# Trainium2, one core: a fused two-block transformer kernel, its opening re-queued and re-ordered, and the forget gates of the second block computed first

## The reference

```
mod = silu(c) @ w_mod + b_mod              # 9 shifts, scales and gates per layer, for x and for ctx
x += 0.5 * gate * swiglu(rms_norm(x) * (1 + scale) + shift)        # and the same for ctx
x += gate * mixing(rms_norm(x) * (1 + scale) + shift)   # Fourier, neighbourhood, gated linear, grouped-query
x += 0.5 * gate * swiglu(...)
```

```
h += out(mixing(rmsnorm(h)))     # 4 softmax pairs with forget gates, 4 retention heads
h += swiglu(rmsnorm(h))
```

## Time and profile before

| | us |
|---|---|
| median of 3 runs (2406.01 to 2409.37) | 2408.04 |
| the profiled execution's own time | 2407.92 |
| its span in the trace | 2405.7 |
| TensorE busy | 2364.2 (98%) |
| VectorE busy | 1536.9 (64%) |
| ScalarE busy | 1013.0 (42%) |
| GpSimd busy | 400.7 (17%) |

### The profile page before, as it was taken

The page is one execution under the profiler, slowest core; times in us unless marked ns, Lnnn a source line. Parts: engine busy times, 40 slices in busy tenths (PEclk is TensorE's granted clock), DMA queues, the critical chain, the costliest instruction groups (busy, mean ns, idle before and its releaser), DMA issues.

```text
span 2405.7 us, 36502 instructions
## 1 busy us (share of the span) xinstructions
PE 2364.2 (98%) x14394; PEld 2047.7 (85%) x14394; DVE 1536.9 (64%) x2617; ACT 1013.0 (42%) x1690; POOL 400.7 (17%) x425
## 2 busy tenths in 40 slices
PE   9999999999999999999999999999999999999998
PEld 6888888777888888888888877999888999899887
DVE  5888765874799855523323585666666665667874
ACT  5222234654522222422223465545345444446663
POOL 2221211340222221111011130121000220000110
PEclk9999999999999999999999999999999999999999
DMA  9566542112366754222222222555433555434554
GB/s 350 193 209 210 179 154 90 62 54 97 126 212 242 242 207 158 88 97 97 96 97 97 90 71 91 183 184 186 150 106 132 176 174 176 144 115 153 189 190 134
DMA packets 97864, 360.75 MB, mean 150 GB/s; under 512 B 11024, under 2 KB 11792, under 8 KB 96544
## 3 DMA queue, kind: packets, MB, share of 16 engines
q1 hardware_dynamic: 75744, 272.84, 33.8%
q0 software_dynamic: 21952, 85.59, 10.0%
HBM read 357.34 MB, written 1.05 MB: 149 GB/s over the span
## 4 chain that ended last, share of the span: by engine, by line
PE 90%; DVE 3%; ACT 3%; issue 2%; DMA 1%; POOL 0%; DVEq 0%; ACTq 0%; POOLq 0%
PE bank L810 25%; PE bank L811 24%; PE bank L812 24%; PE bank L817 6%; PE bank L818 3%; ACT ring_high L1382 1%; PE bank L1162 1%; PE bank L1150 1%; PE bank L1132 1%; DVE ring_low L1883 1%; PE bank L1184 1%; DMA arena<-w_mod_first_dram 1%; PE bank L1111 0%; PE bank L1331 0%; DVE arena L1949 0%
## 5 line engine op out<-in xcount | busy, mean ns | idle before, releaser
L1883 DVE TENSOR_TENSOR ring_low<-ring,ring_high 128x1024 fp32r<-128x1024 f32 x520 | 639.0, 1229 | 508.6 <-ACT ring_high L1382 506.4
L810 PE MATMUL bank<-x_parts,ring_high 128*128 128x512 f32 (+2 forms) x2308 | 802.7, 348 | 6.7 <-DVE x_parts L1958 3.7
L1382 ACT ACTIVATE ring_high<-ring 128x1024 fp32r<-128x1024 f32 x520 | 547.9, 1054 | 585.6 <-PE bank L812 544.7
L812 PE MATMUL bank<-x_parts,ring_low 128*128 128x512 f32 (+2 forms) x2308 | 788.9, 342 | 0.0
L811 PE MATMUL bank<-x_parts,ring_high 128*128 128x512 f32 (+2 forms) x2308 | 787.5, 341 | 0.0
L810 PEld LDWEIGHTS bank<-x_parts,ring_high 128*128 128x128 f32 x2308 | 437.4, 190 | 73.9 <-issue 14.2
L812 PEld LDWEIGHTS bank<-x_parts,ring_low 128*128 128x128 f32 x2308 | 437.3, 189 | 47.6
L811 PEld LDWEIGHTS bank<-x_parts,ring_high 128*128 128x128 f32 x2308 | 437.8, 190 | 46.6 <-issue 1.0
L642 POOL TENSOR_TENSOR hidden_parts<-fresh,hidden_parts 128x512 fp32r<-128x512 f32 (+2 forms) x132 | 203.6, 1542 | 1010.6 <-ACT hidden_parts L1515 1010.6
L1896 DVE CUSTOM_DVE_ANT_0 mod_products<-mod_ring,csilu 128x1024 bf16<-128x1024 f32 x224 | 303.1, 1389 | 32.0 <-DMA mod_ring<-w_mod_dram 30.8
L810 PE MATMUL bank<-hidden_parts,ring_high 128*128 128x512 f32 (+2 forms) x814 | 280.9, 345 | 0.2 <-POOL hidden_parts L642 0.2
(11 more groups left out here) (267 smaller groups left out, 2754.8 us busy)
## 6 DMA issues: line engine op xcount, KB each, us to landing
ring<-stream_dram SPq DMA_DIRECT2D x517, 512.0 KB, 3.3
mod_ring<-w_mod_dram POOLq DMA_DIRECT2D x128, 512.0 KB, 4.5
arena<-w_mod_first_dram POOLq DMA_DIRECT2D x8, 1024.0 KB, 11.8
ring<-stream_dram POOLq DMA_DIRECT2D x3, 512.0 KB, 10.7
arena<-na_bias_dram POOLq DMA_DIRECT2D x2, 768.0 KB, 12.1
mod_ring<-consts_dram POOLq DMA_DIRECT2D x1, 1076.0 KB, 5.4
resid<-x_dram POOLq DMA_DIRECT2D x2, 512.0 KB, 5.9
resid<-ctx_dram POOLq DMA_DIRECT2D x2, 512.0 KB, 7.1
```

Source lines behind the costliest of these rows:

```text
L810: pe.matmul(out, w[0][:, b], xh, start=start, stop=False)
L812: return pe.matmul(out, w[1][:, b], xh, start=False, stop=stop)
L1382: act.activation(high[:, i % SPLIT], ring[:, u % LOADED], ACT.Copy).then_inc(high_parts, 1)
L1883: dve.tensor_tensor(low[:, u % LOADED], ring[:, u % LOADED], high_f[:, i % SPLIT], ALU.subtract).then_inc(low_parts, 1)
```

## The change

1. The two loads of x and the two of ctx move from GpSimd's queue to the sync engine's: x first, then the two small constants, then ctx, then `small`. GpSimd now begins with the first piece of `w_mod`; unit 2 is loaded behind the fourth piece in place of the third.
2. The sums of squares: VectorE adds two pairs for each half as soon as it is squared; TensorE sums the rest, two matmuls for each half in place of one for each token group.
3. ScalarE waits for the mean and makes `rstd` before it copies `first_rows(0)` and splits unit 0; copies for later chunks are one place earlier, behind the high part of the chunk before.
4. TensorE makes the modulation of a chunk two chunks ahead of its products; unit 2's products trail by two chunks.
5. The low part of unit 0 is made on GpSimd, between its DMA issues; VectorE skips it.
6. In the second block the gate's projection is VectorE's first, and the gate's steps come one step (k) earlier on all engines.

```diff
@@ sync
+            for i in range(2):
+                sp.dma_start(resid[:, i * half:(i + 1) * half, META:META + NX], A["x"][:, i * half:(i + 1) * half]).then_inc(
+                    *made(f"x_loaded{i}", i, by=16))
             sp.dma_start(c_cols, ...)
             sp.dma_start(const[:, 0:C_ONES64], ...)
+            for i in range(2):
+                sp.dma_start(resid[:, i * half:(i + 1) * half, META + NX:META + N1], ...)
             sp.dma_start(small, A["small"])...
@@ gpsimd
-            (the four loads of x and ctx)
             for c in range(KC):
...
+                if c == FIRST_SLOTS:
+                    pool.wait_ge(high_parts, 1)
+                    pool.tensor_tensor(low[:, 0], ring[:, 0], high_f[:, 0], ALU.subtract).then_inc(*made("first_unit_low"))
+                if c in (0, 1, 3):
+                    s = min(c, 2)
                     pool.dma_start(ring[:, s], A["stream"][s]).then_inc(*made(f"first_unit_loaded{s}", s, by=16))
@@ tensor, start_units
+                def sums(g, i):
+                    a, b = norm_cols(("start",), g)
+                    pe.wait_ge(*when("first_sums", g, i))
+                    for j in range(2):
+                        mm = pe.matmul(means[:, a:b], cst(C_ONESD), scaled[:, 4 * i + j, a:b],
+                                       start=(i == 0 and j == 0), stop=(i == 1 and j == 1))
+                    return mm
+                sums(0, 0)
+                sums(0, 1)
+                idle_products(1, "ctx_loaded0", 0)
+                sums(1, 0)
+                idle_products(1, "ctx_loaded1", 1)
+                sums(1, 1).then_inc(*made("mean", ("start",)))
                 pe.wait_ge(*when("c_cols_silu", 0))
                 first_modulation(0)
                 idle_products(1, "first_mod_loaded0", 0)
                 first_turn(0)
+                idle_products(3, "first_mod_loaded0", 0)
+                first_modulation(1)
+                idle_products(2, "first_mod_loaded1", 1)
+                first_turn(1)
+                part(0, 0)
+                first_modulation(2)
+                part(1, 0)
+                first_turn(2)
                 for c in range(1, KC):
+                    part(0, c)
+                    part(1, c)
+                    if c + 2 < KC:
+                        first_modulation(c + 2)
+                    if c >= 2:
+                        part(2, c - 2)
+                    if c + 2 < KC:
+                        first_turn(c + 2)
@@ tensor and scalar, second_mixing
-                    if k == SLOT2[FLOG] + 1:
+                    if k == SLOT2[FLOG]:
@@ scalar
+            act.wait_ge(*when("mean", ("start",)))
+            inverse_root(rstd[:, 0], bank("mean", ("start",)), N1, ("start",), ("mean", ("start",)))
             first_rows(0)
             split_ahead(1 - SPLIT)
-            act.wait_ge(*when("mean", ("start",)))
-            inverse_root(rstd[:, 0], bank("mean", ("start",)), N1, ("start",), ("mean", ("start",)))
             first_high(0)
+            first_rows(1)
             split_ahead(1)
             for c in range(1, KC):
-                first_rows(c)
                 first_high(c)
+                if c + 1 < KC:
+                    first_rows(c + 1)
@@ vector, sums of the opening
+                for i in range(2):
+                    dve.wait_ge(*when("first_squares", g, i))
+                    x = scaled[:, 4 * i:4 * i + 4, a:b]
+                    dve.tensor_tensor(x[:, 0:2], x[:, 0:2], x[:, 2:4], ALU.add).then_inc(*made("first_sums", g, i))
@@ vector, forget_gates and second_mixing
-                if k == SLOT2[FLOG] + 1:
+                if k == SLOT2[FLOG]:
...
-                if k == SLOT2[FLOG] + 2:
+                if k == SLOT2[FLOG] + 1:
...
+                    if k == 0:
+                        project(tp, PROJ2, SLOT2[FLOG], N2, proj2, VTEMP2)
+                    if k < len(PROJ2) and k != SLOT2[FLOG]:
                         project(tp, PROJ2, k, N2, proj2, VTEMP2)
```

More of the change, by code:

```diff
@@ L591, in _ @@
         def _(sp):
+            half = KC // 2
+            for i in range(2):
+                sp.dma_start(resid[:, i * half:(i + 1) * half, META:META + NX], A["x"][:, i * half:(i + 1) * half]).then_inc(
+                    *made(f"x_loaded{i}", i, by=16))
             sp.dma_start(c_cols, A["c_cols"].rearrange("p (c s) -> p c s", c=KC)).then_inc(
@@ L594, in _ @@
             sp.dma_start(const[:, 0:C_ONES64], A["consts"][:, 0:C_ONES64]).then_inc(*made("consts_loaded", 0, by=16))
+            for i in range(2):
+                sp.dma_start(resid[:, i * half:(i + 1) * half, META + NX:META + N1],
+                             A["ctx"][:, i * half:(i + 1) * half]).then_inc(*made(f"ctx_loaded{i}", i, by=16))
             sp.dma_start(small, A["small"]).then_inc(*made("small_loaded", 0, by=16))
@@ L716, in flog_weights @@
                 pool.tensor_tensor(flog_w, narrow_raw(u), scale, ALU.mult).then_inc(*made("narrow_scaled", u, 0))
-            half = KC // 2
-            for i in range(2):
-                pool.dma_start(resid[:, i * half:(i + 1) * half, META:META + NX], A["x"][:, i * half:(i + 1) * half]).then_inc(
-                    *made(f"x_loaded{i}", i, by=16))
-            for i in range(2):
-                pool.dma_start(resid[:, i * half:(i + 1) * half, META + NX:META + N1],
-                               A["ctx"][:, i * half:(i + 1) * half]).then_inc(*made(f"ctx_loaded{i}", i, by=16))
             for c in range(KC):
@@ L729, in _ @@
                     *made(f"first_mod_loaded{c % FIRST_SLOTS}", c, by=16))
-                for s in ((0, 1), (), (2,))[c] if c < 3 else ():
+                if c == FIRST_SLOTS:
[3 more added lines that the diff above has]
+                    s = min(c, 2)
                     pool.dma_start(ring[:, s], A["stream"][s]).then_inc(*made(f"first_unit_loaded{s}", s, by=16))
@@ L804, in weights @@
                 unit[0] += 1
-                pe.wait_ge(low_parts, SPLIT_NO[u] + 1)
+                if SPLIT_NO[u]:
+                    pe.wait_ge(low_parts, SPLIT_NO[u])
+                else:
+                    pe.wait_ge(*when("first_unit_low"))
                 return [w.rearrange("p (b n) -> p b n", b=8) for w in (high[:, SPLIT_NO[u] % SPLIT], low[:, u % LOADED])]
@@ L943, in start_units @@
                 means = take("mean", ("start",))
-                idle_products(7, "zeros_set")
+                def sums(g, i):
[5 more added lines that the diff above has]
+                    return mm
+                idle_products(6, "zeros_set")
                 idle_products(2, "x_loaded0", 0)
-                idle_products(3, "x_loaded1", 1)
-                idle_products(2, "ctx_loaded0", 0)
                 pe.wait_ge(*when("consts_loaded", 0))
-                pe.wait_ge(*when("first_sums", 0))
-                pe.matmul(means[:, 0:NX], cst(C_ONESD), sumsq[:, 0:NX], start=True, stop=True)
+                sums(0, 0)
[4 more added lines that the diff above has]
+                sums(1, 1).then_inc(*made("mean", ("start",)))
                 pe.wait_ge(*when("c_cols_silu", 0))
-                idle_products(2, "ctx_loaded1", 1)
                 first_modulation(0)
@@ L955, in start_units @@
                 first_turn(0)
-                pe.wait_ge(*when("first_sums", 1))
-                pe.matmul(means[:, NX:N1], cst(C_ONESD), sumsq[:, NX:N1], start=True, stop=True).then_inc(
-                    *made("mean", ("start",)))
-                for c in range(1, KC):
-                    if c == 1:
-                        idle_products(2, "first_mod_loaded0", 0)
-                    first_modulation(c)
-                    if c == 1:
-                        idle_products(3, "first_mod_loaded1", 1)
-                    if c >= 3:
-                        part(2, c - 3)
-                    first_turn(c)
-                    part(0, c - 1)
-                    part(1, c - 1)
+                idle_products(3, "first_mod_loaded0", 0)
[6 more added lines that the diff above has]
+                first_turn(2)
+                for c in range(1, KC):
+                    part(0, c)
[6 more added lines that the diff above has]
+                        first_turn(c + 2)
                 pe.wait_ge(*when("consts_loaded_rest", 0))
-                for i, c in ((2, 5), (0, 7), (1, 7), (2, 6), (2, 7)):
-                    part(i, c)
+                part(2, KC - 2)
+                part(2, KC - 1)
             def begun(prev):
```

20 lines of the change are left out of this document (6 added, 14 removed).

## The result

The changed kernel takes 2418.83 us (median of 7 runs, 2417.25 to 2420.08), the kernel before 2408.04 in the same comparison (7 runs). The ratio is 1.0043, 95% interval 1.0033 to 1.0054: **slower, by 10.8 us**. The forecast was 2406.6 with a range of 2400.8 to 2413.5. The profiled span grew from 2405.7 to 2417.1 us, by 11.4.

What follows compares the result with a forecast made beforehand. TensorE, busy 98% of the span, was taken as the bound, so only its waits and slow-clock stretches could pay. Gates -5.4 and opening +4.0 summed to -1.4 us: 2406.6 us predicted, range 2400.8 to 2413.5.

Steps and rivals of the forecast that it cites:

- Where T goes: Opening: x and ctx on the sync queue share engines with w_mod in 4 KB packets, landing at 15.1, +4.0 us.
- T: Opening: the landing of ctx's last half, read at the start of its square; 11.13 before, forecast 15.1.
- the second rival: Opening loads: 1 KB packets on the sync queue put T near 22.6, net +6.1 us, 2414; chance 0.17.
- From T to the first product: Opening: norm ready at T + 4.35, first product at T + 10.5 with GpSimd and VectorE blocking each other; T + 10.3 before.
- From the first product on: Opening up to unit 3: TensorE's work stays the same, 27.8 us against 28.0 before.
- The gates: Forget gates in both layers: an earlier gate projection removes L1300's wait and the slow clock behind it, -5.4 us.
- new wait at item 5's turn: Behind the gates: TensorE waits 1.0 us for VectorE's delayed projection of item 5, with the clock staying full.
- Net gain: 1730.17 - 1727.5 = 2.7 us: First layer's gates: TensorE's gain at the turn of item 5, taken as 2.7 us for the second layer too.
- it ends 3.2 - 1.6 = 1.6 us earlier: First layer's gates: VectorE's projection of item 5 ends 1.6 us earlier, at 1727.4.
- gross gain of 8.2: Gates, both layers: 5.21 us of waiting and 3.0 us of slow-clock stretches removed, before any new VectorE wait.
- the first (the sync queue wins): Opening loads: sync queue served first, T 9.5 to 11, -1.6 to 0, gates -5.4 to -7.0: 2401.7; chance 0.28.
- The third, the clock: Opening: TensorE's clock falls after idle times, adding 1.5 to 3 us before the first product: 2409; chance 0.13.

Runs made afterwards that it cites:

- with the loads back: The changed kernel with only the loads of x and ctx back at the head of GpSimd's queue: 2405.72 us, ratio 0.9996.
- the gates alone: The kernel before with only the change's forget-gate part (part 6): 2404.71 us, ratio 0.9991.
- the one that holds its pieces back: The changed kernel, with GpSimd issuing its first piece of w_mod only once ctx's last half has landed: 2408.81 us, ratio 1.0004.
- the loads alone: The kernel before with only the loads of x and ctx moved to the sync queue, x first: 2420.44 us, ratio 1.0057.
- half of x: The mixed opening (old loop, change's sums and norm, earlier gate steps) with only x's first half moved to the sync queue: 2401.19 us, ratio 0.9974.
- the gate steps one place earlier: The kernel before with the forget-gate part, VectorE's gate steps moved one further place earlier: 2400.57 us, ratio 0.9965; second run 2400.69, 0.9972.

## Why the prediction was wrong

**The step that failed** is "Where T goes": "I take 15.1, because the rows show packets in turn and 4 KB". The turns were right and the packets wrong. 4 KB was what GpSimd's queue had made of these loads; on the sync queue they went in 1 KB, the length of the destination's runs. With four times the packets, the same rule gives the second rival's case: T near 22.6, +11.5 us. Measured is 23.98, +12.85, where the forecast had +4.0. The sync-queue loads by themselves cost 13.5 us at the end of the opening, and taking them back returns 13.8. The row that I let decide, 4 KB on the other queue, said nothing of this one. The destination's shape pointed to it, and I gave it 0.17.

**From T to the first product** the walk was right: with the loads back, the norm at T + 4.35 as worked out (Exp ends at 15.55) and the first product at T + 10.1 against T + 10.5. GpSimd's low part took 2.35 us and not 3.1. The 1.54 us that I doubled was a mean over three widths (512 columns took 1.77 us, 256 took 1.22), and the cost doesn't double with the width. VectorE's scaling took 2.90 and not 0.88, and 0.88 again with GpSimd out of the way, so the mutual blocking was real. Against a split on VectorE, which takes its own 1.22 us in front of the scaling, the place on GpSimd cost 0.95. In the changed kernel itself the first product came 1.0 later, at T + 11.13, by the low clock.

**From the first product on** "TensorE's work is the same ... 27.8 us" was off by 1.7: 29.5. The term that was too small is TensorE's wait for the row copies behind ScalarE's high parts, 1.9 us where the kernel before has 0.8; I had put it into the first three chunks, and for less. The rest of the 1.7 stays open. That the shorter norm doesn't pay came out, but GpSimd's low part is only one reason. With that part back on VectorE the first product is 1.1 us earlier than before, and the gain is lost all the same: in the change's order mostly to the row copies, in the old order to unit 1's low part.

**The gates**: L1300's wait gone, the clock behind it full, 1.0 us of new wait at item 5's turn, and 2.7 us gained there in the first layer, all as forecast. Still the part is worth 2.8 us alone (3.2 in the changed kernel) in place of 5.4. The step that failed is "Net gain: 1730.17 - 1727.5 = 2.7 us": the sum stopped at the turn, and took for granted that TensorE keeps what it has there. But from item 5's projection to `x_place` VectorE sets the pace, together with ScalarE, for whose high parts it waits twice in between (1.84 and 2.06 us in both kernels): 11.93 us before (1728.63 to 1740.56), 11.92 after (1741.73 to 1753.65). At the end of such a stretch only VectorE's gain counts, 14.7 - 13.1 = 1.6 us, which I had worked out ("it ends 3.2 - 1.6 = 1.6 us earlier") and not used. The other 1.0 turned into a longer wait for `x_place`. In all six kernels with these gate steps (the changed one, the gates alone, and the four others that keep them) that wait is 2.2 us, TensorE is 1.6 to 1.8 us ahead behind it, and the clock falls to 0.50 within 3 us; what the low clock takes back by 1760 differs, 0.1 to 1.0 us. In the six with the steps one place earlier the wait is 1.3 to 1.5 us and the clock stays full. With the gate steps in VectorE's idle time, 7.8 us come out of the same places, near the gross gain of 8.2 that was worked out.

**The rivals**: the first (the sync queue wins) fell; its 0.28 rested on an argument about the start of x, and x's first half did come early. The third, the clock, came true on the way (0.50 from 15 to 27 us). Up to T it lay in the shadow of the late landing; behind T it cost 1.0 us, where 1.5 to 3 were forecast. Its own cause, a late ctx, is the second rival's. The second was right in place and mechanism, and 4.8 us too small, by T (+1.35), the opening behind it (+2.35) and the gates (+2.2), less 0.5 of drift and 0.6 by which the medians differ less than the two profiled executions. By its own terms the first rival's T is 2.3 + 5.8 + 1.1 = 9.2 and not 9.5, which changes nothing.

## What to carry to other kernels

Before a load is moved to another queue, ask what packets that queue will make of it, and count turns, not bytes. Here the destination's run of 1 KB was the packet on the sync queue and not on GpSimd's, and beside packets of 8 KB the load got a seventh of the other queue's bytes. The packets that the same load has on another queue don't answer the question; a trace of the load in its new place does. When a wait is removed, follow the engine that released it, not the one that waited, to the next place where they meet. What it hasn't gained is waited for again there, and a longer wait can take the clock along, as the 2.2 us did here. Work that an engine has to do early fits into the holes where that engine waits for another; that was worth more here than all of the opening.

## What the runs showed of the hardware

The same four loads of 512 KB went in packets of 4 KB from GpSimd's queue and of 1 KB from the sync engine's, into the same destination. With both queues at work each moved as many packets as the other (154 and 154 in 3 us), whatever their size.

GpSimd's first load is issued at 1.26 us in every kernel here but the one that holds its pieces back. Its first packets came at 3.3 to 3.7 us where the sync queue had only its small loads, and at 4.9 to 5.4 in the three traces (the changed kernel, the loads alone, half of x) where 1 KB packets of x were flowing on it. Why is open.

TensorE's clock falls in places that no kernel here changed, and not in every execution. One kernel (the gate steps one place earlier), profiled twice, shows 1.00 in one and 0.76 in the other from 1404 to 1418 us, with 97 and 73 matmuls there for the same 11.56 us busy:

```profile
1404.00:1418.00 14.00, 11.56 (x97) 8.27 (x97) 13.54 (x30) 9.98 (x24) 7.42 (x10) 1.00 0.24 77
```

```profile
1404.00:1418.00 14.00, 11.56 (x73) 8.75 (x71) 11.55 (x25) 8.80 (x20) 6.52 (x9) 0.76 0.23 74
```

The two spans differ by 2.3 us (2397.1 and 2399.4). A single profile is no measure of a gain of that size; the delay at a landmark on either side of the place is.
